# Where VectorE takes the weight split in a step: at its end instead of its beginning, in a float32 transformer trunk

## The chip, the cores and the metric

The kernel runs on one core of one Trainium2 chip. The metric is the time of one execution on the device in microseconds, as the median of several runs. The core has a matrix engine (TensorE, PE in the profile), VectorE (DVE), ScalarE (ACT), GpSimd (POOL) and SyncE (SP), each with an instruction stream of its own that it works off in order, and 16 DMA engines that move data at the request of such a stream.

## The reference

It is a trunk of two layers over 320 tokens (256 of a prompt, 64 of a sample with states of its own), with 2048 features, all in float32. Layer 0 mixes by retention heads and a multi-scale pool, layer 1 by mLSTM heads. Each is followed by a gated feed-forward part (FFN) with a short convolution. Outputs are the trunk's result and all new states.

```python
def retention_chunk(S, q, k, v, log_gamma):       # 8 heads of 128
    s = einsum('blhd,bmhd->bhlm', q, k) * dec
    intra = einsum('bhlm,bmhe->blhe', s, v)
    inter = einsum('blhd,bhde->blhe', q, S) * q_dec
    S_new = exp(L * log_gamma) * S + einsum('blhd,blhe->bhde', k * k_dec, v)
    return S_new, intra + inter

def trunk(x, ...):
    for l in range(2):
        h = rms_norm(x, norm_mix[l])
        y = retention_pool_mixer(h, ...) if l % 2 == 0 else mlstm_mixer(h, ...)
        x = x + y
        y = conv_ffn(rms_norm(x, norm_ffn[l]), ...)
        x = x + y
    return rms_norm(x, norm_final), states
```

## The kernel before

Activations lie in SBUF with the features on the partitions. All weights of the projections are cut into 770 **units** of 512 KB (512 input features by 256 output features). TensorE multiplies in a fast 32-bit format of less precision, so each float32 operand is split in two: an upper half in that format (`w_hi`, `a` high) and a lower half, the rest (`w_lo`, `a` low). The product is then taken as upper by upper, upper by lower and lower by upper.

A unit goes through four hands, in rings of four slots (`RING = 4`):

1. SP loads it from HBM to `raw` (`load`, line 385). Before that it waits on `lo_ready` until the lower half of the unit four earlier is made (line 388), since only then the slot is free.
2. ScalarE copies `raw` to `w_hi` (`split`, line 885, the copy is line 893), once TensorE has used the unit that had the slot before.
3. VectorE waits on `hi_ready` and subtracts `w_hi` from `raw` into `w_lo` (`split`, line 1300, the subtraction is line 1310), which counts `lo_ready` up.
4. TensorE waits on `lo_ready` (`unit`, line 538) and does the 24 products of the unit (line 549), then counts `unit_used` up.

ScalarE and VectorE work three units ahead of TensorE (`AHEAD = 3`): in the step in which TensorE does unit u, they split unit u + 3. A retention head has eight units and so eight steps (j = 0 to 7), a pool group four, an mLSTM head twelve.

Beside the split each step holds pieces of the head's own work, written out by hand by step number. On VectorE for a retention head: `ret_tail` j = 0 scales V and the gate and transposes V (lines 1418 to 1421), j = 1 places V (line 1426), j = 3 takes the new state, j = 6 makes the mix (lines 1442 to 1445), j = 7 its lower half (line 1449). For the next head `ret_qk` at j = 4 rotates Q and K (lines 1367 to 1376), `ret_turn_k` and `ret_place_k` at j = 5 weigh K by the head's table (line 1403), transpose it and place it (line 1412), `ret_weigh` at j = 7 weighs the scores (lines 1395 to 1398). TensorE does the seven small products of the previous head behind the unit of step 2 (`ret_sums`, line 647; small products are all line 625) and the scores behind that of step 6. `ret_sums` waits among other things for `ret_s0_loaded`, the state that was loaded for the head.

For mLSTM heads VectorE has `ml_steps` and `ml_tail` in the same way: `ml_qk` at j = 4 (lines 1863 to 1885), `ml_place_v` at j = 9 (line 1944), states and variances at j = 11, and TensorE does its products behind the unit of step 10 (`ml_sums`).

**SP's queue** holds all the loads in one order. For retention head h (lines 426 to 435):

```python
with sp.Fori(1, HEADS) as h:
    for j in range(4):
        load(Unit(8 + j, h, 8))
    sp.wait_ge(ret_intra, h)
    sp.dma_start(ret_table, head_row(ret_tables_in, h)).then_inc(ret_table_loaded, 16)
    for j in range(4, 8):
        load(Unit(8 + j, h, 8))
    sp.wait_ge(ret_state, h)
    sp.dma_start(head_row(ret_out, h - 1), s_new).then_inc(ret_stored, 16)
    sp.dma_start(ret_s0, head_row(ret_state_in, h)).then_inc(ret_s0_loaded, 16)
```

The table of head h stands behind the load of unit 8h + 11, which waits for the lower half of unit 8h + 7; VectorE makes it in step j = 4 of the head's own eight steps and uses the table at j = 5. The state of head h stands behind the load of unit 8h + 15, which waits for the lower half of unit 8h + 11; VectorE makes it at j = 0 of the next eight steps, and TensorE uses the state behind the unit of j = 2.

Of the kernel before, what the change touches and what calls it, by code (L numbers as in the profile page):

```python
# [27 lines left out]
AHEAD = RING - 1  # L28
# [3 lines left out]
U_POOL = U_HEADS + HEADS * 8  # L32
# [3 lines left out]
U_ML = U_FFN0 + FFN_UNITS  # L36
U_GATES = U_ML + 4
GATE_UNITS = 2
# [64 lines left out]
@contextmanager  # L103
def counted(engine, trips, per):

    for c, k in per:
        assert c.i is None
        c.base, c.n = c.base + c.n, 0
    with engine.Fori(0, trips) as i:
        for c, k in per:  # L110
            c.i, c.per = i, k
        yield i
    for c, k in per:
        assert c.n == k, (c.sem, c.n, k)
        c.base, c.n, c.i, c.per = c.base + k * trips, 0, None, 0
# [25 lines left out]
def trunk_kernel(nc, x_in, weights, w_pool_in, cols_in, consts_in, ret_tables_in, ret_state_in, ml_state_in,  # L141
                 y_out, ret_out, pool_out, c_out, m_out, conv_out, ffn_out, m_scratch):
    with ExitStack() as ctx:
# [128 lines left out]
        def two(ap, width=T):  # L272
            return ap.rearrange("p (m t) -> p m t", m=2)
# [7 lines left out]
        def high(ap, t):  # L281
            return ap[:, bass.ds(t * 2 * T, T)]

        def low(ap, t):
            return ap[:, bass.ds(t * 2 * T + T, T)]
# [7 lines left out]
        def col(name, i=0, at=0):  # L293
            return cols[:, bass.ds(i + (COL[name] + at), 1)]
# [997 lines left out]
        def _(dve):  # L1292
# [3 lines left out]
            def own():  # L1296

                dve.wait_ge(dve_step, step.value())

            def split(u):  # L1300

                if not u.exists:
                    return
                dve.wait_ge(hi_ready, u.number(1))
                at = u.slot * UW
                if u.i is None and U_GATES <= u.first < U_GATES + GATE_UNITS:
                    r, w = (v[:, at:at + UW].rearrange("p (k c) -> p k c", k=2 * UK)[:, :, P // 2:P] for v in (raw, w_hi))
                    V.tensor_tensor(w, r, w.bitcast(F32), ALU.subtract).then_inc(lo_ready, 1)
                    return
                V.tensor_tensor(w_lo[:, at:at + UW], raw[:, at:at + UW], w_hi[:, at:at + UW].bitcast(F32),  # L1310
                                ALU.subtract).then_inc(lo_ready, 1)
# [9 lines left out]
            def norm(k):  # L1321
                dve.wait_ge(norm_std, k + 1)
                V.reciprocal(rt[:], std[:]).then_inc(rt_ready, 1)
                dve.wait_ge(rt_ready, k + 1)
# [60 lines left out]
            def first_qk_scaled():  # L1385
                dve.wait_ge(qk_raw, 1)
                V.tensor_tensor(q_t, q_t, rt[:], ALU.mult)
                V.tensor_tensor(k_t, k_t, rt[:], ALU.mult).then_inc(qk_ready, 1)
                dve.wait_ge(qk_ready, 1)

            def ret_weigh(h):
                dve.wait_ge(ret_table_loaded, h * 16 + 16)
                dve.wait_ge(ret_scores, h + 1)
                s = ab[:, 2, :]
                V.tensor_tensor(s_t[:, 0:SEQ], s[:, 0:SEQ], ret_table[:, 0:SEQ], ALU.mult)
                V.tensor_tensor(s_t[:, SEQ:SEQ + P], s[:, SEQ:SEQ + P], ret_table[:, 0:P], ALU.mult)
                V.tensor_tensor(s_t[:, SEQ + P:SC], s[:, SEQ + P:SC], ret_table[:, 0:DEC_SEQ], ALU.mult)
                V.tensor_tensor(q_dec, q_t[:, SEQ:T], ret_table[:, SEQ:T], ALU.mult).then_inc(ret_intra, 1)
# [97 lines left out]
            def pool_lower(j):  # L1496
                dve.wait_ge(pool_hi, j + 1)
                for m in range(2):
                    t = HEADS + 2 * j + m
                    V.scalar_tensor_tensor(low(b, t), ab[:, 2 + m, 0:T], col("pool_scale", 0, 2 * (POOL_GROUPS - 1 - j) + m),  # L1500
                                           high(b, t).bitcast(F32), ALU.mult, ALU.subtract).then_inc(b_ready, 1)
# [41 lines left out]
            split(Unit(10))  # L1543

            for j in range(8):
                split(Unit(8 + AHEAD + j))
                if j == 0:
                    norm(0)
                    V.memset(two(pool_ext, EXT)[:, :, 0:POOL_BUF], 0.0)
                    V.memset(k_tok, 0.0)  # L1550
                    V.memset(v_tok, 0.0)
                    first_qk_scaled()
                    V.tensor_tensor(cos_r, con[:, CON["cos"]:CON["cos"] + T], rt[:], ALU.mult)
                    step.inc(V.tensor_tensor(sin_r, con[:, CON["sin"]:CON["sin"] + T], rt[:], ALU.mult))
                    ret_turn_k(0)
                if j == 1:
                    ret_tail(0, 0)
                    ret_place_k(0)
                if j == 2:
                    ret_tail(0, 1)  # L1560
                    ret_weigh(0)
                if j == 3:
                    ret_tail(0, 2)
                if j == 4:
                    ret_tail(0, 3, stored=False)
                if j == 5:
                    own()
                    ret_qk(1, 12)
                    ret_turn_k(1)
                if j == 6:  # L1570
                    ret_place_k(1)
                    ret_tail(0, 6)
                if j == 7:
                    ret_tail(0, 7)
                    ret_weigh(1)
            with counted(dve, HEADS - 2, [(step, 3)]) as i:
                for j in range(8):
                    split(Unit(16 + AHEAD + j, i, 8))
                    ret_tail(i + 1, j)
                    if j == 4:  # L1580
                        ret_qk(i + 2, i * 8 + 20)
                    if j == 5:
                        ret_turn_k(i + 2)
                        ret_place_k(i + 2)
                    if j == 7:
                        ret_weigh(i + 2)
            for j in range(16):
                split(Unit(U_POOL + AHEAD + j))
                ret_tail(HEADS - 1, j)
                if j in (4, 8, 12):  # L1590
                    pool_steps(j // 4 - 1, U_POOL + j)
                if j in (9, 13, 15):
                    pool_lower((9, 13, 15).index(j))

            def out_groups(unit0, pair0, weight, a_base, extra, group, bank=1):

# [404 lines left out]
            def ml_lower(h):  # L2001
                dve.wait_ge(ml_y, h + 1)
                dve.wait_ge(ml_y_hi, h + 1)
                for m in range(2):
                    last = V.scalar_tensor_tensor(low(b, h * 2 + m), o_z[:, m * T:(m + 1) * T],
                                                  col("ml_norm", h * 2, m), high(b, h * 2 + m).bitcast(F32),
                                                  ALU.mult, ALU.subtract)
                last.then_inc(ml_b_ready, 1)

            def ml_tail(h, j):  # L2010
                if j == 0:
                    ml_rs_of(h)
                if j == 2:
                    ml_turn_h(h)
                if j == 3:
                    ml_place_h(h)
                if j == 5:
                    ml_gate(h)
                if j == 10:
                    ml_lower(h)  # L2020
# [62 lines left out]
                if j == 13:  # L2083
                    ml_weigh(0)
            for j in range(12):
                split(Unit(U_ML + AHEAD + GATE_UNITS + 12 + j))
                if j == 0:
                    ml_o(0, U_ML + GATE_UNITS + 12, 0)
                if j == 2:
                    ml_states(0, False)  # L2090
                    ml_var_of(0)
                if j == 3:
                    ml_rs_of(0)
                ml_steps(1, j, U_ML + GATE_UNITS + 12, 1)
                if j == 5:
                    ml_turn_h(0)
                if j == 6:
                    ml_place_h(0)
                if j == 7:
                    ml_gate(0)  # L2100
                if j == 10:
                    ml_lower(0)
            with counted(dve, HEADS // 2 - 1, [(step, 16)]) as i:
                for d in range(2):
                    first = i * 24 + (U_ML + GATE_UNITS + 24 + 12 * d)
                    for j in range(12):
                        split(Unit(U_ML + AHEAD + GATE_UNITS + 24 + 12 * d + j, i, 24))
                        if j == 0:
                            ml_o(i * 2 + (1 + d), first, 1 - d)
                        ml_steps(i * 2 + (2 + d), j, first, d)  # L2110
                        ml_tail(i * 2 + (1 + d), j)

            def extra_c(j):
                if j == 0:
# [192 lines left out]
```

## Time and profile before

| | before |
|---|---|
| median of 3 runs | 2769.65 us (2769.52 to 2770.43) |
| profiled execution | 2770.25 us |
| its span, first to last instruction | 2768.4 us |
| TensorE busy, products | 2748.0 us, 99% |
| VectorE busy | 1947.5 us, 70% |
| ScalarE busy | 1452.4 us, 52% |
| GpSimd busy | 160.7 us, 6% |
| mean rate of the DMA engines | 153 GB/s |
| granted TensorE clock over the span | 0.999 |

TensorE has hardly a gap from start to end. Of the span, the retention heads and the pool stage take about 340 us at the start, and the mLSTM stage lies between about 1350 and 1732 us; the rest are output projections and the two FFN parts. In the views below a row gives first the start in us from the beginning of the span, then its length; idle time of the engine before it stands in brackets with what ended it.

### The profile page before, as it was taken

To read this page: it belongs to the slowest core of one execution; us is meant where nothing else is said; L and a number is where in the kernel's file an instruction comes from. 1 tells how busy PE (TensorE), PEld (TensorE's weight loads), DVE (VectorE), ACT (ScalarE), POOL (GpSimd) and SP (SyncE) were. 2 spreads that over 40 slices of the span, in tenths; PEclk is the share of its full clock that TensorE was granted. 3 is DMA by queue.
4 is the path that set the end of the run, shared out by engine and by line. 5 is a ranking of instruction groups with operands and counts; after the bars stand their busy time and mean duration, and the time that the engine had idled before them with its cause. 6 is when DMAs were issued, how large, how long until landed. Compare 5 with 4: busy or idle time off the path is not lost.

```text
span 2768.4 us, 44064 instructions
## 1 busy us (share of the span) xinstructions
PE 2748.0 (99%) x15343; PEld 2496.2 (90%) x15343; DVE 1947.5 (70%) x3203; ACT 1452.4 (52%) x2442; POOL 160.7 (6%) x134
## 2 busy tenths in 40 slices
PE   9999999999999999999999999999999999999998
PEld 8999988888888888888999999888888888888887
DVE  8877667676567665668887778667675667655776
ACT  6555345665355543555555556546654455535554
POOL 0000032000000000002300000330000000000004
PEclk9999999999999999999999999999999999999999
DMA  6444345454545454544544444444444444444443
GB/s 239 153 155 152 124 137 163 143 165 140 168 142 163 144 166 140 165 142 149 161 149 147 153 147 153 139 147 152 157 147 159 146 159 148 154 162 145 152 149 127
DMA packets 121143, 422.64 MB, mean 153 GB/s; under 512 B 13720, under 2 KB 18848, under 8 KB 120864
## 3 DMA queue, kind: packets, MB, share of 16 engines
q1 hardware_dynamic: 120416, 419.75, 46.6%
q8 instruction: 120, 1.97, 0.3%
q10 hardware_dynamic: 576, 0.66, 0.1%
q14 instruction: 31, 0.25, 0.0%
HBM read 414.22 MB, written 6.14 MB: 152 GB/s over the span
## 4 chain that ended last, share of the span: by engine, by line
PE 93%; DVE 4%; ACT 2%; DMA 1%; issue 1%; ACTq 0%; SPq 0%; DVEq 0%
PE gb L589 38%; PE gb L599 25%; PE gb L549 18%; PE ab L559 10%; PE ab L625 2%; DVE w_lo L1310 1%; ACT w_hi L893 1%; DMA x<-in_x 0%; ACT work L1027 0%; DMA work<-in_ret_tables 0%; DVE a L1317 0%; DMA work<-in_ret_state 0%; DVE work L1443 0%; DVE work L1481 0%; DVE work L2147 0%
## 5 line engine op out<-in xcount | busy, mean ns | idle before, releaser
L1310 DVE TENSOR_TENSOR w_lo<-raw,w_hi 128x1024 fp32r<-128x1024 f32 x767 | 951.2, 1253 | 512.9 <-ACT w_hi L893 508.0
L893 ACT ACTIVATE w_hi<-raw 128x1024 fp32r<-128x1024 f32 x769 | 809.9, 1058 | 874.4 <-PE gb L599 417.9
L589 PE MATMUL gb<-a,w_hi 128*128 128x512 f32 x2816 | 684.0, 390 | 0.0
L549 PE MATMUL gb<-a,w_hi 128*128 128x320 f32 x2800 | 622.8, 311 | 1.6 <-DVE a L1317 0.6
L589 PEld LDWEIGHTS gb<-a,w_hi 128*128 128x128 f32 x2816 | 525.0, 188 | 105.4
L549 PEld LDWEIGHTS gb<-a,w_hi 128*128 128x128 f32 x2800 | 467.3, 188 | 5.1 <-DVE a L1317 1.4
L589 PE MATMUL gb<-b,w_hi 128*128 128x512 f32 x1920 | 464.6, 390 | 0.0
L549 PE MATMUL gb<-a,w_lo 128*128 128x320 f32 x1400 | 432.7, 309 | 0.0
L599 PE MATMUL gb<-a,w_lo 128*128 128x320 f32 x2816 | 426.8, 309 | 0.0
L599 PEld LDWEIGHTS gb<-a,w_lo 128*128 128x128 f32 x2816 | 419.8, 188 | 6.8
L589 PEld LDWEIGHTS gb<-b,w_hi 128*128 128x128 f32 x1920 | 358.1, 188 | 71.8
L1027 ACT ACTIVATE work<-work 32x128 f32<-32x128 f32 x960 | 295.9, 308 | 207.9 <-DVE work L1334 197.1
L599 PE MATMUL gb<-b,w_lo 128*128 128x320 f32 x1920 | 292.4, 309 | 0.0
L599 PEld LDWEIGHTS gb<-b,w_lo 128*128 128x128 f32 x1920 | 286.8, 188 | 5.3
L549 PEld LDWEIGHTS gb<-a,w_lo 128*128 128x128 f32 x1400 | 262.8, 188 | 0.0
L509 POOL TENSOR_TENSOR sq_one<-x 128x320 f32 x60 | 70.8, 1180 | 2574.8 <-DVE x L1358 2563.8
L559 PE MATMUL ab<-w_hi,a 128*128 128x512 f32 x704 | 188.6, 390 | 0.6 <-ACT w_hi L893 0.6
L559 PEld LDWEIGHTS ab<-w_hi,a 128*128 128x128 f32 x704 | 131.8, 188 | 29.0 <-ACT w_hi L893 1.9
L559 PE MATMUL ab<-w_hi,b 128*128 128x512 f32 x480 | 128.8, 390 | 0.3 <-ACT w_hi L893 0.3
L559 PEld LDWEIGHTS ab<-w_hi,b 128*128 128x128 f32 x480 | 89.5, 188 | 19.3 <-DVE b L1702 0.7
L1646 DVE TENSOR_TENSOR work<-gb,rt 128x384 f32<-128x384 f32 x44 | 24.6, 559 | 104.9 <-PE gb L589 104.9
L1356 DVE TENSOR_TENSOR x<-gb,x 128x640 f32 (+1 forms) x63 | 51.9, 824 | 63.6 <-PE gb L589 53.2
(216 smaller groups left out, 1656.1 us busy)
## 6 DMA issues: line engine op xcount, KB each, us to landing
raw<-in_weights SPq DMA_DIRECT2D x769, 512.0 KB, 3.5
work<-in_ret_tables SPq DMA_DIRECT2D x8, 320.0 KB, 3.8
out_c<-work SPq DMA_DIRECT2D x8, 257.0 KB, 4.9
x<-in_x SPq DMA_DIRECT2D x3, 640.0 KB, 7.4
work<-m_scratch SPq DMA_DIRECT2D x8, 192.0 KB, 4.9
out_y<-work SPq DMA_DIRECT2D x3, 480.0 KB, 3.5
work<-in_ml_state SPq DMA_DIRECT2D x8, 128.5 KB, 4.7
work<-in_w_pool SPq DMA_DIRECT2D x1, 1024.0 KB, 7.2
```

Source lines behind the costliest of these rows:

```text
L509: step.inc(nc.gpsimd.tensor_tensor(sq_one[:], tile(x, t), tile(x, t), ALU.mult))
L549: last = nc.tensor.matmul(bank(b, m), w[:, at:at + P], v, start=kg == k == n == 0, stop=kg == groups - 1 and k == UK - 1 and n == 2)
L559: last = nc.tensor.matmul(out, act[:, t:t + P], w[:, :, k, :], start=q == k == 0, stop=q == quads - 1 and k == UK - 1)
L589: last = nc.tensor.matmul(gb[:, 2 * p + m, :], w_hi[:, at:at + P], act[:, t:t + 512], start=q == k == 0, stop=final and low_first and k == ...
L599: last = nc.tensor.matmul(bank(p, m), w_lo[:, at:at + P], act[:, t:t + T], start=False, stop=final and not low_first and k == UK - 1)
L625: return nc.tensor.matmul(out, lhs, rhs, start=start, stop=stop)
L893: nc.scalar.activation(w_hi[:, at:at + UW], raw[:, at:at + UW], ACT.Copy).then_inc(hi_ready, 1)
L1027: last = nc.scalar.activation(left_t_blocks[feats * 32:(feats + 1) * 32, :, tokens, :], left_blocks[tokens * 32:(tokens + 1) * 32, :, feat ...
L1310: V.tensor_tensor(w_lo[:, at:at + UW], raw[:, at:at + UW], w_hi[:, at:at + UW].bitcast(F32), ALU.subtract).then_inc(lo_ready, 1)
L1356: step.inc(V.tensor_tensor(two(tiles(x, p * 2)), banks(b), two(tiles(x, p * 2)), ALU.add))
L1646: V.tensor_tensor(two(low_gate)[:, :, 0:WIDE_LO], lows_of(0), r[:, :, 0:WIDE_LO], ALU.mult)
```

## The change

In the VectorE stream alone, the call `split(Unit(...))` moves from the first place in the body of a step to its last. It concerns the first eight-step loop of the retention heads, the counted loop of the heads, the 16 steps of the last head and the pool, the first twelve-step loop of the mLSTM heads and their counted loop. The splits and their order among themselves stay the same, as do the streams of SP, ScalarE, GpSimd and TensorE. The first mLSTM loop (14 steps), the output projections and the FFN parts are left as they are.

```diff
--- before.py
+++ after.py
@@ -1543,7 +1543,6 @@
             split(Unit(10))
 
             for j in range(8):
-                split(Unit(8 + AHEAD + j))
                 if j == 0:
                     norm(0)
                     V.memset(two(pool_ext, EXT)[:, :, 0:POOL_BUF], 0.0)
@@ -1573,9 +1572,9 @@
                 if j == 7:
                     ret_tail(0, 7)
                     ret_weigh(1)
+                split(Unit(8 + AHEAD + j))
             with counted(dve, HEADS - 2, [(step, 3)]) as i:
                 for j in range(8):
-                    split(Unit(16 + AHEAD + j, i, 8))
                     ret_tail(i + 1, j)
                     if j == 4:
                         ret_qk(i + 2, i * 8 + 20)
@@ -1584,13 +1583,14 @@
                         ret_place_k(i + 2)
                     if j == 7:
                         ret_weigh(i + 2)
+                    split(Unit(16 + AHEAD + j, i, 8))
             for j in range(16):
-                split(Unit(U_POOL + AHEAD + j))
                 ret_tail(HEADS - 1, j)
                 if j in (4, 8, 12):
                     pool_steps(j // 4 - 1, U_POOL + j)
                 if j in (9, 13, 15):
                     pool_lower((9, 13, 15).index(j))
+                split(Unit(U_POOL + AHEAD + j))
 
             def out_groups(unit0, pair0, weight, a_base, extra, group, bank=1):
 
@@ -2083,7 +2083,6 @@
                 if j == 13:
                     ml_weigh(0)
             for j in range(12):
-                split(Unit(U_ML + AHEAD + GATE_UNITS + 12 + j))
                 if j == 0:
                     ml_o(0, U_ML + GATE_UNITS + 12, 0)
                 if j == 2:
@@ -2100,15 +2099,16 @@
                     ml_gate(0)
                 if j == 10:
                     ml_lower(0)
+                split(Unit(U_ML + AHEAD + GATE_UNITS + 12 + j))
             with counted(dve, HEADS // 2 - 1, [(step, 16)]) as i:
                 for d in range(2):
                     first = i * 24 + (U_ML + GATE_UNITS + 24 + 12 * d)
                     for j in range(12):
-                        split(Unit(U_ML + AHEAD + GATE_UNITS + 24 + 12 * d + j, i, 24))
                         if j == 0:
                             ml_o(i * 2 + (1 + d), first, 1 - d)
                         ml_steps(i * 2 + (2 + d), j, first, d)
                         ml_tail(i * 2 + (1 + d), j)
+                        split(Unit(U_ML + AHEAD + GATE_UNITS + 24 + 12 * d + j, i, 24))
 
             def extra_c(j):
                 if j == 0:
```

## Rows read from the trace of the kernel before

**Rows 1.** page, part 1 and part 5 (busy us, mean ns, idle before, releaser)

```profile
PE 2748.0 (99%) x15343; PEld 2496.2 (90%) x15343; DVE 1947.5 (70%) x3203; ACT 1452.4 (52%) x2442; POOL 160.7 (6%) x134
...
L1310 DVE TENSOR_TENSOR w_lo<-raw,w_hi 128x1024 fp32r<-128x1024 f32 x767 | 951.2, 1253 | 512.9 <-ACT w_hi L893 508.0
```

**Rows 2.** waits of TensorE, 41 to 341 us (who <- for whom: us, times, longest)

```profile
PE ab L625 <- DVE b L1449: 0.6, 1, 0.6
PE ab L625 <- DVE work L1398: 0.4, 1, 0.4
```

**Rows 3.** waits of TensorE, 1395 to 1750 us

```profile
PE ab L625 <- DVE work L1944: 1.2, 1, 1.2
PE ab L559 <- ACT w_hi L893: 0.3, 1, 0.3
```

**Rows 4.** chain that ended last, 55 to 100 us (start, us, what)

```profile
61.04 5.20 DMA work<-in_ret_tables
...
78.06 4.22 DMA work<-in_ret_state
...
82.41 2.01 PE ab L625 x14
```

**Rows 5.** timeline of ScalarE, 119.0 to 119.4 us

```profile
119.31 1.06 ACT L893 ACTIVATE w_hi<-raw 128x1024 fp32r<-128x1024 f32 x1 [4.23 <-PE gb L549]
```

**Rows 6.** timeline of TensorE, 144.9 to 147.2 us

```profile
145.18 1.93 PE L625 MATMUL ab<-work 128*128 128x256 f32 x14
```

**Rows 7.** timeline of VectorE, 99 to 134 us

```profile
103.47 0.48 DVE L1449 TENSOR_TENSOR b<-work,b 128x320 f32 x1
...
104.67 1.22 DVE L1310 TENSOR_TENSOR w_lo<-raw,w_hi 128x1024 fp32r<-128x1024 f32 x1
105.81 0.48 DVE L1418 TENSOR_TENSOR work<-gb,rt 128x320 f32<-128x320 f32 x1
...
106.72 0.51 DVE L1421 STREAM_TRANSPOSE work<-work 128x320 f32<-128x320 f32 x1
...
120.41 1.23 DVE L1310 TENSOR_TENSOR w_lo<-raw,w_hi 128x1024 fp32r<-128x1024 f32 x1 [3.61 <-ACT w_hi L893]
121.55 0.48 DVE L1367 TENSOR_TENSOR work<-gb,work 128x320 f32<-128x320 f32 x1
...
125.60 1.23 DVE L1310 TENSOR_TENSOR w_lo<-raw,w_hi 128x1024 fp32r<-128x1024 f32 x1
126.74 0.48 DVE L1403 TENSOR_TENSOR work<-work 128x320 f32<-128x320 f32 x1
...
133.69 1.22 DVE L1310 TENSOR_TENSOR w_lo<-raw,w_hi 128x1024 fp32r<-128x1024 f32 x1
```

**Rows 8.** timeline of SP, 99 to 134 us

```profile
107.13 0.33 SPq L435 DMA_DIRECT2D work<-in_ret_state  x1
...
122.33 0.33 SPq L430 DMA_DIRECT2D work<-in_ret_tables  x1
```

**Rows 9.** line 430, the tables' loads, all seven

```profile
DMA to landing us min/median/max: 3.6/3.8/5.2
```

**Rows 10.** line 435, the states' loads, all seven

```profile
DMA to landing us min/median/max: 3.1/3.2/4.2
```

**Rows 11.** timeline of VectorE, 20 to 106 us

```profile
49.30 1.18 DVE L1310 TENSOR_TENSOR w_lo<-raw,w_hi 128x1024 fp32r<-128x1024 f32 x1
50.40 0.48 DVE L1418 TENSOR_TENSOR work<-gb,rt 128x320 f32<-128x320 f32 x1
...
53.60 1.22 DVE L1310 TENSOR_TENSOR w_lo<-raw,w_hi 128x1024 fp32r<-128x1024 f32 x1
```

**Rows 12.** timeline of TensorE, 53.2 to 54 us

```profile
53.65 0.46 PE L549 MATMUL gb<-a,w_hi 128*128 128x320 f32 x2
```

**Rows 13.** timeline of VectorE, 1522 to 1572 us

```profile
1567.34 1.22 DVE L1310 TENSOR_TENSOR w_lo<-raw,w_hi 128x1024 fp32r<-128x1024 f32 x1
```

**Rows 14.** timeline of TensorE, 1569.9 to 1570.9 us

```profile
1570.57 0.54 PE L549 MATMUL gb<-a,w_hi 128*128 128x320 f32 x2
```

## The prediction, made blind

> **What bounds the kernel now.** I read the page first: TensorE has work in 99% of the span and VectorE in 70% [rows 1]. So a time can fall only by what TensorE waits for, and rise only if somebody comes too late for TensorE. The same rows show what the change aims at: in front of the weight split (line 1310) VectorE sat idle 512.9 us in all, nearly all of it until ScalarE's upper half was there. Next I read TensorE's own waits in the stages that change. They are few: two in the retention heads and the pool stage, 1.0 us together [rows 2], and in the mLSTM stage 1.2 us for the placing of V (line 1944) and 0.3 us for an upper half in the first quad behind it [rows 3]. That is all there is to win, about 2 us. VectorE's idle time is not on TensorE's path.
>
> So the question is what the later split releases later. It releases two things: TensorE's unit three steps on (a wide margin), and SP's queue. SP waits for a lower half before each load of a raw unit, and two loads stand in that same queue behind such a wait: the retention table of the next head and the state `ret_s0`. The chain of waits for the first heads shows them as links already: table issued at 61.04, 5.20 us to land, then VectorE's work, then the state issued at 78.06, 4.22 us, and only then TensorE's seven products (line 625) at 82.41 [rows 4].
>
> **One steady head, step by step.** I take the head from 103 to 146 us and count steps J0 to J7 of the VectorE loop (line 1577). The split of step Jn is that of the unit three further on.
>
> Before: step J4 begins when TensorE releases it, which is when ScalarE starts its upper half at 119.31 [rows 5]. VectorE's split starts at 120.41 and ends at 121.64; SP issues raw unit and table, the table at 122.33, 0.69 us behind the split's end [rows 7, 8]. It takes 3.8 us (median [rows 9]) and is there at 126.1. VectorE comes to it (line 1403) at 126.74 [rows 7]. So the table is hidden, by 0.6 us only, and what hides it is ret_qk, which runs between the split and line 1403 (121.55 to 125.60: 4.05 us).
>
> After: ret_qk comes first and the split behind it, so that the table is asked for when the work that hid it is over, and line 1403 is the next thing in VectorE's in-order queue. The new chain from 119.31: ret_qk 4.05, split 1.22 (end 124.6), SP 0.69, table 3.8, wake-up 0.13 (TensorE's from 82.28 to 82.41 in [rows 4]): line 1403 starts at 129.2 instead of 126.74. VectorE is idle for 4.6 us. Behind it is queued, without a gap, everything up to the next head: turning and placing K, a split, and the mix (126.74 to 133.69: 6.95 us), a split (1.14 from start to next start, 120.41 to 121.55), lower half and weighing (103.47 to 104.67: 1.20), a split (1.14), V and gate with the transpose (105.81 to 107.23: 1.42), and the split of J0 (1.22) [rows 7]. Sum 13.07: that split ends at 142.3. Before, it ended at 105.89 in the head before this one, and the heads repeat every 31.4 us: 137.2. On it hangs the state: SP issues it 1.24 us after the split's end (105.89 to 107.13 [rows 7, 8]), it takes 3.2 us [rows 10], and TensorE wakes 0.13 later: 146.8. TensorE itself is ready for these products at 145.18 [rows 6]. That is a stall of 1.66 us. With the shortest landings (3.6 and 3.1) it is 1.4. **I take 1.5 us a head.** TensorE's stall moves the next J4 by the same amount, so the chain starts again from there and nothing is made up: the stall comes back at each head. The chain runs from J4 of a pass of the loop to step J2 of the next, for heads 2 to 7 (the last one in the pool stage): 6 x 1.5 = **+9.0 us**.
>
> All other deadlines on this chain hold: the splits come up to 6 us later than before and end about 1 to 2 us ahead of their unit; were one missed, TensorE would wait there and correspondingly less at the state, since the chain counts from J4 in either case. The mix's upper half still has a split to cover it. The raw loads behind later splits land within 3.5 us and are wanted a step or more later.
>
> **The first head.** Here VectorE has hardly a gap. The reciprocal no longer has a split ahead of it (0.6 earlier), but split 11 (1.14) and the work of J1, `ret_tail` and placing K (50.40 to 53.60: 3.2 us), now stand ahead of split 12, which started at 49.30 [rows 11]. It starts at 53.0 and ends at 54.3; TensorE wants the unit at 53.65 [rows 12]. That stall of 0.7 replaces the 0.4 for line 1398 [rows 2]. Then table 1, issued at 61.04 [rows 4]: its split now stands behind the copy of the state, which waits for TensorE's products, and I put it 1.1 us later, at 62.1. With 4.8 us to land (between 3.8 and 5.20), 0.13, the work of 13.07 as above and 1.24 the state is issued at 81.3 instead of 78.06 [rows 4]; with 3.2 to 4.22 to land TensorE starts at about 85.0 instead of 82.41. **+2.5 us** for all of this (2.0 to 3.2).
>
> **Pool stage.** The lower half of head 7 (line 1449) comes ahead of its split instead of behind it: TensorE's 0.6 us for it goes [rows 2], **-0.6**. What is late next there (pool_hi, the pooled products) has steps of room.
>
> **mLSTM heads.** The first loop loses its wait for line 1944: V is placed before the split of its step, not after it: **-1.2** [rows 3]; next late is ScalarE's half of the placing, about a microsecond ahead of the products. In the steady heads I find no new wait. The longest work now ahead of a split is ml_qk in J4; before, the split of J5 stood directly behind it, at 1567.34 [rows 13], so the split of J4 ends by 1568.6 at the latest and its unit runs from 1570.57 [rows 14]. State and m row are loaded behind the split of J3, whose step holds only copies that wait for ScalarE anyway: no later than before. At the end one split (up to 1.14 us, less the 0.3 that VectorE waited there) comes between the last variance and line 1988, and TensorE's wait for ScalarE's upper half [rows 3] hangs on that chain: **+0.8** (bounds 0 and 1.1).
>
> **Sum.** 9.0 + 2.5 - 0.6 - 1.2 + 0.8 = +10.5. The profiled execution took 2770.25 us with a span of 2768.4; the median is 2769.65, 0.6 less. A stall adds to either alike: 2769.65 + 10.5 = **2780.2 us**.
>
> The Trainium skill ("DMA: Bandwidth & Descriptors", section "Anatomy of one DMA — SWDGE (gpsimd) path") speaks against this result: a fit, made for the other issue path, of about 2.0 us plus the bytes at 436 GB/s. For 320 KB and 64 KB that is 2.75 and 2.15 us (estimates from that page), 2.1 us less in the two links than the rows; the steady stall would vanish and the time be about 2771. The rows decide here: both loads stand right behind a 512 KB load in one queue.
>
> **Rivals.**
> (a) The chain closes in time and the steady stall is absent. It is 1.5 us out of a chain of 27; the page's fit above would do it, or loads that land together sooner by 1.5 us than their medians. Against it: in all seven heads no table took less than 3.6 [rows 9], and the order of the queue is fixed. It gives 2769.65 + 1.5 = 2771.2.
> (b) Faster: none of these loads comes too late and all TensorE waits on VectorE go: 0.6 + 0.4 + 1.2 = 2.2, so 2767.5. Even that is within 0.2% (5.5 us, about what a measurement of this kernel can tell from no change).
> (c) The loads take what they took in the first head: 5.20 and 4.22 [rows 4] instead of 3.8 and 3.2. Each steady head then stalls 2.4 us more: 6 x 2.4 = 14.4, which gives 2794.6. For it: these are real landings of the same loads; against it: they met the 1024 KB of the pool weights and bunched raw loads.
>
> **Chances.** The forecast (stall 0.8 to 2.2 us a head, 2776 to 2785): 0.70. (a) 0.14, (b) 0.03, (c) or something between 0.11; 0.02 for a gain of over 5.5 us that I see no source for. Faster 0.02, same 0.17, slower 0.81. The range reaches to the edge of (a) and a little towards (c): 2772 to 2788.
>
> **What would show it.** After the change: a wait of VectorE line 1403 on the table, some 4 to 5 us, seven times; waits of TensorE line 625 on the load of ret_state, seven times, 1 to 3 us each; a head's period of 32.9 us instead of 31.4; line 1449 and 1944 gone from TensorE's waits; the mLSTM heads with unchanged period; FFN stages unchanged. VectorE's idle time for ScalarE's upper half falls by a good part, without any gain. I am wrong if TensorE has no wait on ret_state, if the table's load lands before VectorE asks for it, or if the steady mLSTM heads grow.

## The result

| | before | after |
|---|---|---|
| median | 2769.59 us (6 runs, 2768.92 to 2770.43) | 2783.75 us (6 runs, 2780.01 to 2788.38) |
| ratio, 95% interval | | 1.0052 (1.0042 to 1.0063) |
| span of the profiled execution | 2768.4 us | 2783.0 us |

The changed kernel is 14.2 us slower, half a per cent. The forecast was 10.5 us slower, 2780.2, with a range (2772 to 2788) that holds the median; the slowest of the six runs, 2788.38, lies just above it. Busy times on the page hardly change; VectorE's idle time ahead of the split, 512.9 us before [rows 1], is 87 us less and bought nothing:

```profile
PE 2751.6 (99%) x15343; PEld 2497.5 (90%) x15343; DVE 1948.8 (70%) x3203; ACT 1453.5 (52%) x2442; POOL 160.7 (6%) x134
...
L1310 DVE TENSOR_TENSOR w_lo<-raw,w_hi 128x1024 fp32r<-128x1024 f32 x767 | 950.8, 1252 | 425.6 <-ACT w_hi L893 420.8
```

TensorE's waits from 41 to 360 us (who, for whom: us, times, longest) are all new ones. Where [rows 2] had VectorE's lines 1449 and 1398, there are now the state's load and, for less, three lower halves:

```profile
PE ab L625 <- DMA work<-in_ret_state: 11.3, 7, 2.5
PE gb L549 <- DVE w_lo L1310: 1.9, 3, 1.1
```

VectorE's waits in the same stretch begin with the table, which cost 0.5 us in the whole kernel before:

```profile
DVE work L1403 <- DMA work<-in_ret_tables: 32.0, 7, 6.2
```

This is one steady head of the changed kernel on VectorE's timeline (start, length, engine, line; idle time before it in brackets). It answers to [rows 7], and J4 begins here at 126.82:

```profile
126.82 0.49 DVE L1367 TENSOR_TENSOR work<-gb,work 128x320 f32<-128x320 f32 x1 [3.09 <-PE gb L549]
...
130.87 1.22 DVE L1310 TENSOR_TENSOR w_lo<-raw,w_hi 128x1024 fp32r<-128x1024 f32 x1
136.64 0.49 DVE L1403 TENSOR_TENSOR work<-work 128x320 f32<-128x320 f32 x1 [4.54 <-DMA work<-in_ret_tables]
...
143.59 1.22 DVE L1310 TENSOR_TENSOR w_lo<-raw,w_hi 128x1024 fp32r<-128x1024 f32 x1
...
148.41 1.18 DVE L1310 TENSOR_TENSOR w_lo<-raw,w_hi 128x1024 fp32r<-128x1024 f32 x1
```

and SP's and TensorE's timelines for it:

```profile
132.27 0.33 SPq L389 DMA_DIRECT2D raw<-in_weights  x1
132.79 0.33 SPq L430 DMA_DIRECT2D work<-in_ret_tables  x1
...
150.84 0.33 SPq L435 DMA_DIRECT2D work<-in_ret_state  x1
```

```profile
154.10 0.45 PE L625 MATMUL ab<-work 128*128 128x256 f32 x1 [1.26 <-DMA work<-in_ret_state]
```

The chain can be followed link by link. ret_qk ends, the split runs from 130.87 to 132.09, SP issues raw unit and table behind it, and VectorE stands still for 4.54 us until the table is there. Without a gap all other work follows up to the split of J0 at 148.41; the state is issued at 150.84 and TensorE gets it at 154.10. From the start of J4 to TensorE's products it is 27.3 us; in [rows 5, 6] it was 25.9.

### The profile page after: what moved, and what is told of

It reads as the page before. It is cut to its first block, busy times and chain, and to the rows that moved or that the text cites. A ratio compares the mean times of both kernels' runs of the same rounds, so it can differ in the third digit from the quotient of the medians.

```text
span 2783.0 us, 44064 instructions
## 1 busy us (share of the span) xinstructions
PE 2751.6 (99%) x15343; PEld 2497.5 (90%) x15343; DVE 1948.8 (70%) x3203; ACT 1453.5 (52%) x2442; POOL 160.7 (6%) x134
## 4 chain that ended last, share of the span: by engine, by line
PE 88%; DVE 6%; DMA 2%; issue 1%; ACT 1%; SPq 0%; DVEq 0%; ACTq 0%
PE gb L589 38%; PE gb L599 24%; PE gb L549 14%; PE ab L559 10%; PE ab L625 2%; DVE w_lo L1310 2%; DMA work<-in_ret_tables 1%; DMA work<-in_ret_state 1%; DVE work L1443 1%; ACT w_hi L893 0%; DVE work L1412 0%; ACT work L1027 0%; DMA x<-in_x 0%; DVE work L1367 0%; DVE work L1369 0%
## 5 line engine op out<-in xcount | busy, mean ns | idle before, releaser
L1356 DVE TENSOR_TENSOR x<-gb,x 128x640 f32 (+1 forms) x63 | 51.9, 824 | 63.6 <-PE gb L589 53.2
```

The lines of the kernel that those rows point to most:

```text
L1356: step.inc(V.tensor_tensor(two(tiles(x, p * 2)), banks(b), two(tiles(x, p * 2)), ALU.add))
```

## Experiments

The theory is that of the prediction, called the queue theory: what costs time is the place of two loads in SP's queue, behind waits for lower halves that now come later. "By the products' positions" means here: by the time between TensorE's groups of products of line 625, which stand at the same places of every kernel's stream, in one trace against another. The rivals: TensorE gets its own lower halves too late (late splits); VectorE's idle time for the table costs by itself; each moved split adds its share; or the loss lies in the mLSTM heads as well. Each run was timed against the kernel before on the same chip.

| kernel | median us | ratio to before (95%) |
|---|---|---|
| e1, changed, both loads early | 2768.14 | 0.9995 (0.9986 to 1.0005) |
| e2, changed, state early | 2770.13 | 1.0003 (0.9994 to 1.0013) |
| e3, changed, table early | 2769.76 | 1.0001 (0.9991 to 1.001) |
| e4, changed, but J4 as before | 2772.69 | 1.0014 (1.0004 to 1.0024) |
| e5, before, J4 alone moved | 2770.58 | 1.0004 (0.9995 to 1.0013) |
| e6, mLSTM part alone | 2769.04 | 0.9998 (0.9989 to 1.0007) |
| e7, retention and pool part alone | 2786.16 | 1.0061 (1.0045 to 1.0076) |
| e8, changed, state one load later | 2815.05 | 1.0166 (1.015 to 1.0181) |
| e9, e1 with three splits put back | 2766.2 | 0.9988 (0.9979 to 0.9997) |
| e10, before, both loads early | 2769.04 | 0.9998 (0.9989 to 1.0007) |

The median of before was 2769.38 to 2769.43 beside them.

**e1: both loads earlier in SP's queue, all splits as in the changed kernel.**

```diff
             with sp.Fori(1, HEADS) as h:
-                for j in range(4):
+                for j in range(2):
                     load(Unit(8 + j, h, 8))
                 sp.wait_ge(ret_intra, h)
                 sp.dma_start(ret_table, ...)
+                for j in range(2, 4):
+                    load(Unit(8 + j, h, 8))
+                sp.wait_ge(ret_state, h)
+                sp.dma_start(... s_new ...)
+                sp.dma_start(ret_s0, ...)
                 for j in range(4, 8):
                     load(Unit(8 + j, h, 8))
-                sp.wait_ge(ret_state, h)
-                sp.dma_start(... s_new ...)
-                sp.dma_start(ret_s0, ...)
```

> The changed kernel, with both loads earlier in SP's queue: the table behind the second raw load of the head instead of the fourth, the state (with the store before it) behind the fourth instead of the eighth. Queue theory (the stalls come from two loads that stand in SP's queue behind late splits): no wait of VectorE line 1403 on the table, no wait of TensorE line 625 on ret_state; 2768 to 2770 us. Rival, late splits (TensorE loses by getting its own lower halves too late, since the splits are up to 6 us later): the splits are where they were, so about 2780 or more remains. Rival, clock (the stretch at lower clock costs in any case): some 1.5 us stay.

It took 2768.14 us: the whole loss is gone, with no split moved back. VectorE has no wait for the table, and of TensorE's waits between 41 and 360 us one is left, for the lower half of unit 12 (lines are two further down here):

```profile
PE gb L551 <- DVE w_lo L1312: 0.5, 1, 0.5
```

So the moved splits cost nothing by their place in the program. But in time they are no longer late: counted from the split of J4, those of J5 to J0 start 4.6 us sooner here than in the changed kernel, since VectorE doesn't wait for the table. Whether late splits cost by themselves is therefore left to e2. The clock's rival falls: the stretch at lower clock (below) is gone with the waits, and the granted clock from 41 to 360 us is 1.00.

**e2: the state alone early**, directly behind the table, the table where it was.

```diff
                 sp.dma_start(ret_table, ...)
-                for j in range(4, 8):
-                    load(Unit(8 + j, h, 8))
                 sp.wait_ge(ret_state, h)
                 sp.dma_start(... s_new ...)
                 sp.dma_start(ret_s0, ...)
+                for j in range(4, 8):
+                    load(Unit(8 + j, h, 8))
```

> The changed kernel with the state alone earlier in SP's queue: directly behind the table, ahead of the raw loads 4 to 7 of the head. Queue theory: VectorE keeps its wait of 4 to 6 us for the table, seven times, and its splits stay as late as in the changed kernel, but TensorE doesn't wait for ret_state; what is left is waits of TensorE on w_lo where a table takes over 4.6 us to land, 1 to 3 us in all: 2769 to 2773. Rival, VectorE's lost time or late splits cost by themselves: about 2780 or more.

2770.13 us. This is the sharpest of the runs. VectorE's and then TensorE's waits from 41 to 360 us:

```profile
DVE work L1403 <- DMA work<-in_ret_tables: 32.9, 7, 6.2
```

```profile
PE gb L549 <- DVE w_lo L1310: 0.8, 2, 0.5
```

VectorE stands still for the table as long as in the changed kernel (32.9 against 32.0 us), and TensorE waits 0.8 us instead of 13.2. From the products at 41 us to the products of the last head the trace is 1.2 us longer than before by the products' positions, against 16.6 us for the changed kernel. So VectorE's idle time and its late splits together cost about 1 us; it is the state behind them that cost the rest.

**e3: the table alone early**, behind the head's second raw load; the state stays last.

```diff
-                for j in range(4):
+                for j in range(2):
                     load(Unit(8 + j, h, 8))
                 sp.wait_ge(ret_intra, h)
                 sp.dma_start(ret_table, ...)
+                for j in range(2, 4):
+                    load(Unit(8 + j, h, 8))
                 for j in range(4, 8):
                     load(Unit(8 + j, h, 8))
```

> The changed kernel with the table alone earlier in SP's queue (behind the second raw load of the head). Queue theory: VectorE has no wait for the table, so all splits of J5 to J0 come 4 to 5 us sooner, and the state, still last in the queue, is there 2 to 3 us before TensorE wants it: 2768 to 2770. If the state's place in the queue costs by itself, waits on ret_state of about 1.5 us stay and the time is about 2778.

2769.76 us. VectorE has no wait for the table, and TensorE's waits for the state come to 0.5 us, once, in the first head:

```profile
PE ab L627 <- DMA work<-in_ret_state: 0.5, 1, 0.5
```

The state's place hardly costs by itself either: it takes both, the table that holds VectorE up and the state that hangs on VectorE's last split.

**e4: the changed kernel, but in the heads' counted loop the split of j = 4 comes first.**

```diff
                 for j in range(8):
+                    if j == 4:
+                        split(Unit(16 + AHEAD + j, i, 8))
                     ret_tail(i + 1, j)
 ...
-                    split(Unit(16 + AHEAD + j, i, 8))
+                    if not (j == 4):
+                        split(Unit(16 + AHEAD + j, i, 8))
```

> The changed kernel, but in the counted loop of the retention heads the split of step j = 4 stays at the beginning; all others stay moved. Queue theory: the table's load is issued by 122.3 on the scale of the kernel before and lands 0.5 us after VectorE wants it; the state lands about a microsecond ahead of TensorE's products; what stays is the first head's share (it lies mostly ahead of that loop), about 2 to 3.5 us, less 0.6 and 0.6 won: 2769 to 2773. Rival, the sum of all moved splits makes the stall (each adds its share): an eighth of it goes, about 2781.

2772.69 us, 3.3 above before. One split of the eight takes 11 of the 14 us away. In its trace the steady heads have no stall; the wait for the state is there once, in the first head, whose steps lie ahead of the counted loop:

```profile
PE ab L625 <- DMA work<-in_ret_state: 2.0, 1, 2.0
```

The 3.3 us that stay are of the first head: by the products' positions it is 3.1 us longer than before, and behind its stall stands a stretch at lower clock (0.56 from 86.4 to 90.0 us) that costs 1.6; about 1.5 are won in the pool and mLSTM stages. The rival of equal shares expected 2781.

**e5: the converse, the kernel before with the split of j = 4 alone moved** (the edit of e4 with the condition turned round).

> The kernel before with one split moved: that of step j = 4 in the counted loop of the retention heads, behind ret_qk. Queue theory: the table is asked for 3 us later and VectorE waits for it some 3 to 4.5 us in each of six heads, but without V and gate ahead of the split of J0 the state's load is issued at about 141 on the scale of the kernel before and lands about a microsecond ahead of TensorE's products at 145.18: no stall, 2769 to 2771. Rival, any wait of VectorE for the table reaches TensorE: 6 times 1 us or more, 2776 or more.

2770.58 us; the interval of the ratio holds 1. VectorE waits for the table in all six heads and TensorE's waits from 41 to 350 us are those of the kernel before (VectorE's row first):

```profile
DVE work L1403 <- DMA work<-in_ret_tables: 23.4, 6, 4.7
```

```profile
PE ab L625 <- DVE b L1449: 0.6, 1, 0.6
PE ab L625 <- DVE work L1398: 0.4, 1, 0.4
```

Neither J4's split alone (e5) nor the others without it (e4) make the chain too long in the steady heads. The margin counted out for e5 was about a microsecond, and it was enough.

**e6 and e7: the two halves of the change.** e6 has the moves of the two mLSTM loops alone, e7 those of the retention loops and the pool stage alone (the hunks of the diff ahead of the prediction).

> The kernel before with the moves in the two mLSTM loops alone. Theory: TensorE's wait for line 1944 goes (-1.3), its wait for the upper half in the first quad of the output projection grows (+0.7), the steady heads keep a period of 46.6 us: 2768.6 to 2769.4. Rival, the moved splits delay the loads of the state and the m row in the mLSTM heads too: a wait of TensorE or of VectorE's line 1914 in each head, 2772 or more.

> The kernel before with the moves in the retention heads and the pool stage alone. Theory: all of the loss is here and the mLSTM part gives 0.6 back, so this is 0.6 over the changed kernel: 2781 to 2788. Rival, the loss is shared with the mLSTM stage: clearly below 2780.

e6 took 2769.04, e7 2786.16 us. The loss is all in the retention half. In the trace of e6 TensorE's wait for line 1944 is gone, its waits for upper halves behind the last head have grown, and no mLSTM head has a new one, against the rival of late m rows; from 1390 to 1750 us these are left:

```profile
PE ab L559 <- ACT w_hi L893: 0.8, 2, 0.5
PE ab L625 <- DVE work L1928: 0.3, 1, 0.3
```

e7 lies 2.4 us over the changed kernel, 0.6 was expected; the changed kernel's own runs spread by more than that (last section).

**e8: the cause made larger.** The state, with the store ahead of it, goes behind one more raw load, that of the next head's first unit; all else stays.

```diff
+            load(Unit(16))
             with sp.Fori(1, HEADS) as h:
-                for j in range(4):
+                for j in range(1, 4):
                     load(Unit(8 + j, h, 8))
                 sp.wait_ge(ret_intra, h)
                 sp.dma_start(ret_table, ...)
-                for j in range(4, 8):
+                for j in range(4, 9):
                     load(Unit(8 + j, h, 8))
                 sp.wait_ge(ret_state, h)
 ...
-            loads(first, 8)
+            for j in range(1, 8):
+                load(Unit(first + j))
             sp.wait_ge(ret_state, HEADS)
```

> The changed kernel with the cause made larger: the state's load (and the store before it) one raw load later in SP's queue, behind the first raw load of the next head, which waits for the split of J1. Nothing else changes. Queue theory: between the splits of J0 and J1 stand the placing of V and one split, 2.9 us, so each of seven stalls on ret_state grows by 2.9 us: about 2804 (2800 to 2808). Rival, late splits or VectorE's idle time cost the time and the state's load is there only by coincidence: no more than 2 or 3 us over the changed kernel. Clock: stalls of 4 to 5 us instead of 1 to 2.5; where a stretch at lower clock follows each of them, up to 1.5 us a head more, 2810 or more.

2815.05 us, above the 2800 to 2808 of the queue theory alone and in the part that was expected with a lower clock behind each stall. TensorE's waits from 41 to 400 us:

```profile
PE ab L627 <- DMA work<-in_ret_state: 31.8, 7, 4.9
PE gb L551 <- DVE w_lo L1312: 0.8, 2, 0.5
```

31.8 against 11.3 us in the changed kernel: 2.9 a head, as worked out from the work between the two splits. The rest of the 31 us is the clock. These are stretches around the second head's stall: from and to, length, busy us and number of instructions of PE, its weight loads, DVE, ACT and POOL, then the granted clock (1.00 is 2.4 GHz, 0.5 is 1.2 GHz), the DMA engines' share and GB/s:

```profile
110.00:121.70 11.70, 11.35 (x75) 10.72 (x74) 11.47 (x24) 6.53 (x14) 0.00 (x0) 1.00 0.49 168
121.70:126.60 4.90, 0.05 (x1) 0.01 (x1) 2.14 (x3) 2.28 (x3) 0.00 (x0) 1.00 0.74 215
126.60:130.30 3.70, 3.68 (x16) 3.59 (x17) 0.18 (x1) 0.00 (x0) 0.00 (x0) 0.56 0.24 94
130.30:159.00 28.70, 28.70 (x195) 28.49 (x195) 21.39 (x46) 14.65 (x28) 0.00 (x0) 1.00 0.33 114
```

TensorE waits 4.9 us, and the 3.7 us after it run at 0.56 of the clock. A lower clock stands behind all seven stalls. Behind the first it lasts longest (0.50 from 86.3 to 90.0 us, 0.59 from there to 93.5) and costs 3.1 us by the products' positions, behind the six others about 1.6 to 1.7 each: some 13 us together, where the changed kernel has 1.5.

**e9: what is left, repaired.** e1, with the splits of j = 0 and 1 of the first retention loop and of j = 11 of the counted mLSTM loop back at the beginning of their steps.

```diff
             for j in range(8):
+                if j < 2:
+                    split(Unit(8 + AHEAD + j))
                 if j == 0:
                     norm(0)
 ...
-                split(Unit(8 + AHEAD + j))
+                if j >= 2:
+                    split(Unit(8 + AHEAD + j))
 ...
                     for j in range(12):
+                        if j == 11:
+                            split(Unit(U_ML + AHEAD + GATE_UNITS + 24 + 12 * d + j, i, 24))
 ...
-                        split(Unit(U_ML + AHEAD + GATE_UNITS + 24 + 12 * d + j, i, 24))
+                        if j != 11:
+                            split(Unit(U_ML + AHEAD + GATE_UNITS + 24 + 12 * d + j, i, 24))
```

> The changed kernel with both loads early as in e1, and two splits back at the beginning of their steps: j = 0 and 1 of the first retention loop, and j = 11 of the mLSTM loop. Theory: against e1 TensorE's wait of 0.7 us for unit 12 goes, and its wait for the upper half behind the last mLSTM head shrinks back by 0.7: 2766.3 to 2767.2. If those two are not the causes, 2768.1 stays.

2766.2 us, 0.1 under the expected range, below the kernel before with an interval that narrowly leaves 1 out (0.9979 to 0.9997), and 1.9 below e1. TensorE has no wait left between 41 and 360 us, and from 1390 to 1750 us these (lines shifted by up to five):

```profile
PE ab L627 <- DVE work L1933: 0.3, 1, 0.3
PE ab L561 <- ACT w_hi L895: 0.2, 1, 0.2
```

It is the fastest of all, 3.2 us below the kernel before. By the products' positions 0.6 of them are won at the wait for line 1398, 0.4 at the state's load of the first head, 0.8 at line 1449 and 1.4 at line 1944.

**e10: the kernel before with both loads early** (the edit of e1 made there), to see whether e1's time comes from that alone.

> The kernel before, only with both loads early in SP's queue as in e1: what the early loads alone are worth. Theory: the kernel before has 0.3 us of wait on ret_state and nothing else hangs on them: 2769.0 to 2769.4. So e1's gain over it is that of the moved splits.

2769.04 us, the same as before within the interval. The early loads are worth next to nothing where almost nothing hangs on them (0.3 us in the first head by the products' positions); in the changed kernel they are worth 15.6 us. Against e10 the order of the splits in e9 gains 2.8 us.

## Why the prediction was right, step by step

**Bound and winnings.** TensorE's waits were all there was to win, and about 2 us for them was somewhat low: e9 won 3.2. The products behind a wait start later than the wait alone explains, and the 0.4 at the first head's state were not counted. The prediction also left out one wait of TensorE in the mLSTM stage, 0.3 us for line 1928, which stays in every run. VectorE's idle time in [rows 1] was not on TensorE's path: the changed kernel has 87 us less of it and gained nothing by that, and in e2 and e5 VectorE's 33 and 23 us at the table cost TensorE about 1 us and nothing.

**The steady head.** The chain was put at line 1403 9.9 us behind the start of J4 and at TensorE's products 27.5 behind it by medians; measured in the head above 9.8 and 27.3. Predicted idle time for the table 4.6 us, measured 4.54. The stall was put at 1.5 us a head; the waits of TensorE on the state in heads 2 to 7 are 1.7, 1.3, 1.5, 2.5, 1.0 and 0.9, mean 1.5. In this head the margins ahead of TensorE's units held too: the lower half started at 143.59 ends 0.8 us before TensorE's first product of its unit. The period of heads 2 to 7 was put at 32.9 us and is 32.5 to 34.4.

**The first head.** Predicted +2.5, measured +3.7 by the products' positions. The mis-sized term is the table's landing: 4.8 us taken, 5.91 measured. In the same stretch the wait for unit 12 was there as predicted (0.7; 0.5 in the trace, 0.7 by the products' positions of e1 against e9). With the later table unit 17 waited for its lower half, 1.1 us. The prediction had worked out such deadlines for the steady heads alone.

**The second head and what is missing from the sum.** Heads 2 to 7 were put at 9.0 us and measured at 12.9. The stalls themselves make 8.9. The table of head 2 took 5.52 us, and with it units 24 and 25 waited for their lower halves (0.5 us in the trace, 1.0 by the products' positions): that all other deadlines on the chain hold failed in this head. The products behind each stall start some 0.2 us later than the wait alone explains (about 1.5 us in six heads), and 1.5 us were not in the prediction at all: the clock. These are stretches of the changed kernel with the products behind the stall of head 2 (columns as for e8):

```profile
119.70:121.50 1.80, 1.79 (x14) 1.75 (x15) 0.89 (x1) 0.57 (x1) 0.00 (x0) 0.97 0.78 280
121.50:125.00 3.50, 3.50 (x15) 3.50 (x15) 1.68 (x3) 0.00 (x0) 0.00 (x0) 0.53 0.53 163
125.00:154.10 29.10, 27.84 (x190) 27.39 (x188) 21.64 (x45) 16.86 (x31) 0.00 (x0) 1.00 0.40 128
```

For 3.5 us TensorE has 0.53 of its clock and starts 15 products where in the kernel before the same length holds 27:

```profile
115.50:119.00 3.50, 3.50 (x27) 3.50 (x26) 1.30 (x3) 0.00 (x0) 0.00 (x0) 1.00 0.76 260
```

That the median stayed within the narrower 2776 to 2785 us owes something to chance: the chain was right, but some 5 us of the profiled run are terms that the sum had too small or not at all, and two of the six runs (2787.6 and 2788.4) lie above it.

**Pool and mLSTM.** Predicted -0.6, -1.2 and +0.8. By the products' positions: -0.8 for line 1449, -1.4 for line 1944, +0.8 for the upper half behind the last head. The wait of the last is named in the traces of the changed kernel and of e6 (0.5 us), and e9 takes it away with the split that made it. All terms together are 15.2 us; the profiled execution is 14.6 longer, as it reached the products at 41 us 0.7 sooner than the one before. In the twelve traces that point lies anywhere between 40.5 and 42.3 us. The steady mLSTM heads keep their period of 46.6 us.

**Rivals.** (a), a chain that closes in time, is what the steady heads of e4 and all heads of e5 show; with the whole change it did not. (b), faster, needed the loads out of the way and three splits put back, and then gave 2766.2 (e9), 1.3 under the 2767.5 worked out for it. (c), the long landings of the first head in every head, happened in heads 1, 2 and 5 only (5.91, 5.52 and 4.58 us; else 3.55 to 3.83).

**Landings and issue.** The state's load took 2.9 to 3.7 us in the changed kernel and the table's 3.5 to 5.9. The fit of the Trainium skill ("DMA: Bandwidth & Descriptors", section "Anatomy of one DMA — SWDGE (gpsimd) path"), made for the other issue path, gave estimates of 2.15 and 2.75 and with them no steady stall; the measurement decides. The same section of the Trainium skill says that a DMA's wait for a semaphore happens on the issuing sequencer ahead of dispatch. The trace agrees: SP issued the raw unit 0.2 us after the split's end (132.09 to 132.27), and the table 0.5 behind that, though the scores that it waits for had been weighed in the head before. That is why a load's place in the queue, and not its own condition, decided when it went out.

## What to carry to other kernels

Before an instruction is moved within an in-order stream, list everything that waits for its semaphore, and then everything that stands behind that waiter in its queue: here the split's reader TensorE had over 6 us of room in the steady heads, while two loads behind SP's wait had 0.6 and 3.5 us. Where a load is asked for by one engine's progress and hidden by the same engine's work, its cover is the work between the two, and moving that work across removes it without any dependence showing it. A load whose data is wanted soon belongs early in its queue, at the place where its own condition is met; then the order of the splits was free here (e1), and small waits could be won (e9).

## What the runs showed that was not expected

TensorE's clock can fall after stalls that are short. In the changed kernel a wait of 1.7 us in head 2, behind smaller ones for units 24 and 25, was followed by 3.5 us at 0.53 (1.5 us lost); the stalls of 2.4 and 2.5 us in heads 1 and 5 were not. In e4 the one stall of 2.0 us was followed by 3.6 us at 0.56 (1.6 lost); in e7 the first head's stall of 3.3 us by 3.6 us at 0.62, while the 1.9 us in head 2 were not. In e8 each of seven stalls of over 4 us was followed by such a stretch, 3.1 us lost behind the first and 1.6 to 1.7 behind the others. The changed kernel's runs spread over 8 us where those of before spread over 1.5, and the slower ones have the lower clock: of its six runs four have a mean granted clock of 0.998 and take 2780.0 to 2784.8 us, two have 0.996 and take 2787.6 and 2788.4. Why one short stall brings it and another doesn't stays open; no run here separates it.
